# Collecting the scores of five scan levels in one column range: 80 predicated copies become 20, with three additions at level 6

## The reference

```
def step(s, inp):                      # one chunk of the prompt
    qc, kc, vc, gc = inp
    b = jnp.cumsum(gc, axis=2)
    diff = b[:, :, :, None, :] - b[:, :, None, :, :]
    decay = jnp.exp(jnp.where(tri[:, :, None], diff, NEG_BIG))
    att = jnp.einsum('bhtd,bhsd,bhtsd->bhts', qc, kc, decay)
    o = (jnp.einsum('bhts,bhsv->bhtv', att, vc)
         + jnp.einsum('bhtd,bhdv->bhtv', qc * jnp.exp(b), s))
```

## Time and profile before

| | us |
|---|---|
| median of 3 executions | 2847.42 (2844.85 to 2847.95) |
| the profiled execution, its own time | 2846.17 |
| its span, first to last instruction | 2844.4 |
| PE busy in the span | 2810.3 (99%) |
| DVE, ACT, POOL busy | 1689.4, 950.6, 1596.5 |
| granted TensorE clock, mean | 0.997 |

### The profile page before, as it was taken

One profiled execution on the slowest core, in us unless ns is written; L12 is line 12 of the kernel. 1 busy time (PEld: TensorE's weight loads), 2 busy tenths in 40 slices (PEclk: granted clock), 3 DMA queues, 4 the chain that ended last, 5 costly groups with the idle time before them and its releaser, 6 DMA issues.

```text
span 2844.4 us, 63198 instructions
## 1 busy us (share of the span) xinstructions
PE 2810.3 (99%) x24828; PEld 2766.3 (97%) x24828; DVE 1689.4 (59%) x2419; ACT 950.6 (33%) x1616; POOL 1596.5 (56%) x1466
## 2 busy tenths in 40 slices
PE   8999999999999999999999999999999999999998
PEld 7999999999999999999999999999999999999998
DVE  8554677545553578383784637766454446783645
ACT  4221233123152425151452414330412523452433
POOL 6666676556654674525464352766565556734343
PEclk9999999999999999999999999999999999999999
DMA  5796835665654655353444433355665557453532
GB/s 191 199 247 191 237 101 182 170 154 155 185 167 111 189 163 162 117 175 110 126 144 140 156 120 109 121 169 169 160 181 153 161 151 186 148 170 118 158 123 78
DMA packets 196956, 444.27 MB, mean 156 GB/s; under 512 B 13464, under 2 KB 57664, under 8 KB 195904
## 3 DMA queue, kind: packets, MB, share of 16 engines
q1 hardware_dynamic: 107360, 281.09, 30.4%
q0 software_dynamic: 40128, 125.83, 18.7%
q10 hardware_dynamic: 49248, 34.28, 4.0%
HBM read 422.64 MB, written 144.35 MB: 199 GB/s over the span
## 4 chain that ended last, share of the span: by engine, by line
PE 93%; DVE 3%; ACT 1%; POOL 1%; issue 1%; ACTq 0%; DVEq 0%; PEld 0%; POOLq 0%
PE dense L723 60%; PE SA L783 15%; PE SB L783 11%; POOL Wl L588 1%; PE SA L998 1%; PE SA L915 1%; PE SA L859 1%; PE SA L1001 1%; PE SA L903 1%; PE SA L846 0%; PE SA L920 0%; POOL Wh L586 0%; PE SB L1005 0%; PE SA L848 0%; PE SA L855 0%
## 5 line engine op out<-in xcount | busy, mean ns | idle before, releaser
L588 POOL TENSOR_TENSOR Wl<-raw,Wh 128x512 fp32r<-128x512 f32 x620 | 854.0, 1377 | 51.8
L586 POOL TENSOR_SCALAR Wh<-raw 128x512 fp32r<-128x512 f32 x620 | 450.9, 727 | 672.8 <-PEq L728 445.8
L723 PE MATMUL dense<-Hh,Wh 128*128 128x272 f32 x2768 | 585.8, 293 | 15.2 <-POOLq L590 10.1
L723 PE MATMUL dense<-Hh,Wl 128*128 128x272 f32 x2768 | 573.9, 289 | 0.5 <-issue 0.5
L723 PE MATMUL dense<-Hl,Wh 128*128 128x272 f32 x2768 | 572.6, 288 | 0.0
L723 PEld LDWEIGHTS dense<-Hh,Wh 128*128 128x128 f32 x2768 | 435.0, 189 | 25.7 <-issue 16.2
L723 PEld LDWEIGHTS dense<-Hl,Wh 128*128 128x128 f32 x2768 | 436.7, 189 | 0.0
L723 PEld LDWEIGHTS dense<-Hh,Wl 128*128 128x128 f32 x2768 | 434.0, 189 | 0.8 <-issue 0.8
L651 POOL TENSOR_TENSOR Sl<-pair,Sh 128x512 fp32r<-128x512 f32 x120 | 173.7, 1465 | 421.8 <-ACT Sh L1088 421.0
L723 PE MATMUL dense<-Ah,Wh 128*128 128x272 f32 x1408 | 291.9, 289 | 0.8 <-DVE X L1814 0.7
L723 PE MATMUL dense<-Al,Wh 128*128 128x272 f32 x1408 | 290.7, 288 | 0.0
(11 more groups left out here) (473 smaller groups left out, 6317.4 us busy)
## 6 DMA issues: line engine op xcount, KB each, us to landing
raw<-wst SPq DMA_DIRECT2D x276, 512.0 KB, 3.7
w_sums<-wst POOLq DMA_DIRECT2D x36, 1536.0 KB, 13.3
w_sums<-wst POOLq DMA_DIRECT2D x18, 2048.0 KB, 16.8
pair<-wst SPq DMA_DIRECT2D x120, 256.0 KB, 3.5
pair<-w_sums SPq DMA_DIRECT2D x60, 512.0 KB, 3.7
wsum<-w_sums SPq DMA_DIRECT2D x60, 512.0 KB, 3.6
w_sums<-w_sums POOLq DMA_DIRECT2D x12, 1536.0 KB, 9.0
wsum<-wst SPq DMA_DIRECT2D x60, 256.0 KB, 2.5
```

What stands on the lines that cost most here:

```text
L586: pool.tensor_scalar(Wh[:, j, cs], raw[:, j, cs], 1.0, 0.0, ALU.mult, ALU.add).then_inc(glink, 1)
L588: pool.tensor_tensor(Wl[:, j, cs], raw[:, j, cs], f32(Wh[:, j, cs]), ALU.subtract).then_inc(glink, 1)
L723: mm = pe.matmul(out[:, a, 0:HALF], w[:, ring, w0:w0 + 128], x[:, k, a * HALF:(a + 1) * HALF], start=(k == 0 and n == 0), stop=(k == nk - ...
```

## The change

Levels 1 to 5 no longer write to the four diagonal 32x32 blocks. One predicated copy on all 128 partitions writes all four groups' scores into the last 32 columns (96 to 127) of each block of `attC`. The last group of partitions has its diagonal block there already. At level 6, before its own copies, three additions of 32 partitions x 16 blocks x 32 columns add what groups 0 to 2 have collected to their diagonal blocks, where step `d` has written the diagonal; a sync of the chain stands behind them, since level 6 overwrites part of the collecting range. The mask that one copy needs must stand in the same 32 columns for all partitions, so three copies in `layer_bounds` of the first layer (32 partitions x 5 levels x 32 columns of bytes) bring the top-left mask block down to the other groups.

```diff
             def layer_bounds(L):
+                for j in range(1, 4 if L == 0 else 1):
+                    low, all_ = (lvm[g, 0:5 * P].rearrange("p (l t) -> p l t", t=P)[:, :, 0:32]
+                                 for g in (slice(0, 32), slice(32 * j, 32 * j + 32)))
+                    ch.did(dve.tensor_copy(all_, low))
                 ch.link(dve.tensor_copy(lbc[:, 0:4].unsqueeze(1), lbs[:, L:L + 1, :]))
...
                 elif kind == "lv":
                     dve.sem_inc(dve_began, 1)
                     bs, hf = 1 << h, 1 << (h - 1)
+                    for g in (slice(32 * j, 32 * j + 32) for j in range(3 if hf == 32 else 0)):
+                        ch.did(TT(attC[g, :, g], attC[g, :, g], attC[g, :, 96:P], ALU.add))
+                    if hf == 32:
+                        ch.sync()
                     for s0 in range(0, CH if hf >= 32 else 0, bs):
...
-                    for j in range(4 if hf < 32 else 0):
-                        g = slice(32 * j, 32 * j + 32)
+                    if hf < 32:
                         ch.did(dve.copy_predicated(
-                            attC[g, :, g].rearrange("p c (n b) -> p c n b", b=bs)[:, :, :, hf:bs],
-                            mask(h)[g, g].rearrange("p (n b) -> p n b", b=bs)[:, :, hf:bs].unsqueeze(1).to_broadcast(
-                                [32, HEADS * NCH, 32 // bs, hf]),
-                            SA[g, 0, 0:HEADS * NCH * 16].rearrange("p (c n b) -> p c n b", c=HEADS * NCH, b=hf)))
+                            attC[:, :, 96:P].rearrange("p c (n b) -> p c n b", b=bs)[:, :, :, hf:bs],
+                            mask(h)[:, 0:32].rearrange("p (n b) -> p n b", b=bs)[:, :, hf:bs].unsqueeze(1).to_broadcast(
+                                [P, HEADS * NCH, 32 // bs, hf]),
+                            SA[:, 0, 0:HEADS * NCH * 16].rearrange("p (c n b) -> p c n b", c=HEADS * NCH, b=hf)))
```

## The result

The changed kernel takes 2859.75 us (median of 6 runs, 2857.40 to 2861.42), the kernel before 2847.51 beside it. The ratio is 1.0038, 95% interval 1.0024 to 1.0051: slower, by about 12 us. The profiled execution has 2860.03 us, its span is 2858.2.

What follows compares the result with a forecast made beforehand. PE was taken to bound the kernel, busy 2810.3 of 2844.4 us. The terms -1.4 + 0.6 + 9.4 + 3.0 = +11.6 us, on 2847.42, gave 2859.0 us, range 2848 to 2866.

Steps and rivals of the forecast that it cites:

- Level 6 against POOL: Additions at level 6 push DVE's last three instructions into POOL's work; PE waits 2.2 and 2.5 us before level 7: +9.4 us.
- Levels 4 and 5: Shorter predicated copies let DVE finish before PE asks; the four waits of levels 4 and 5 in scan 0 go: -1.4 us.
- The mask copies: At about 121 us, first copy sits out POOL's block, three at 0.2 us follow while PE waits: +0.6 us.
- the lower of my two workings: Scan 1, level 6: old 2.64 us plus 1.5 for POOL's company, a 2.4 us wait; turn by turn 3.3.
- The clock: Behind the new waits ahead of level 7, PE at half clock in two of four cases: +3.0 us, bounds 0 and 6.
- The no-change rival: At level 6 only the additions' overrun of 0.6 and 0.35 us stays: 2848.5 us; chance 0.20.
- the waits without clock loss: Rival: the waits ahead of level 7 come but no half clock behind them: +8.6 us, 2856.0 us; chance 0.30.
- the wide copy as dear as four: Rival: one wide copy costs as much as four, levels 4 and 5 keep their 1.4 us: 2860.4 us; chance 0.06.

## Why the prediction was right

The forecast was 2859.0 us, +11.6; measured are 2859.75 and +12.2 of the medians (7 to 15 by the interval). The mechanism held. That the two numbers lie within 1 us of each other is in part luck. The profiled pair is 13.9 us apart, not 12.2. I had 12.4 us for what the additions cost (waits and clock) and 0.8 for what the rest gives back; by the medians the additions cost 14.3 us (from the kernel without them to the changed one) or 16.3 (put alone into the kernel before), and the rest gives back 2.1 to 4.1. Both sizes were too small, and their errors offset each other.

- **Level 6 against POOL** was the step that carried the sum, and it held: 9.4 us forecast, 9.0 measured, 1.97 in scan 0 and 2.55 in scan 1 for my 2.2 and 2.5. That the additions' own time isn't the cause is shown by two of them, which fit the margin and still cost 4.9 us of waits. The rule that I cited from the Trainium skill (SBUF — State Buffer, "Who interferes with whom") agrees with the turns in the timelines above: in scan 0, POOL's L588 of 578.70 lasts 2.13 us through L1953, and L1956 behind it 2.30. The turns are read from starts and ends; no run moved POOL's work itself. One detail of my working was off: the first addition of scan 1 would be blocked for 0.57 us; there, POOL had come earlier and DVE later, and the three additions lost 0.08. In turn POOL's company cost the last three lines of scan 1 2.04 us (4.68 for 2.64), where the lower of my two workings had 1.5. That the total came out the same was luck.
- **Levels 4 and 5**: -1.4 forecast, -1.0 measured; one wait of 0.44 stayed. The wide copy costs what a narrow one did (median 0.45 us for both):

```profile
L2022 DVE COPY_PREDICATED att<-lvm,SA x20: 435/452/746, 525.6 to 2145.9; 128x256 f32<-128x256 uint8 x20
```

- **The mask copies**: +0.6 forecast, 0.8 measured. The first sat out POOL's L588 (1.37 us), the two others took 0.25 each, as one line's min/median/max shows:

```profile
L1638 DVE COPY lvm<-lvm x3: 250/252/1368, 121.0 to 122.6; 32x160 uint8<-32x160 uint8 x3
```

- **The clock** was the term of least ground: two stretches of four (+3.0) forecast; three came, and with what went and came elsewhere the profile has +5.1. The stretches at 1848 and 2312 us of the profile after have no new wait ahead of them, and others of that kind come and go between kernels that don't differ there; I had no term for them. I had only the size of the wait to go by, and the size doesn't decide: half clock came behind the wait of 1.97 us at 1988 us and not behind the one of 1.96 us at 583 us, and behind both waits of 2.55 us here and neither of those in the kernel with each wide copy four times. In the kernel with two additions, whose longest wait was 1.42 us, it came behind none of the four.
- **The no-change rival** fell with the waits of 9.0 us (its bound was 6.5) and with the two-additions kernel; **the waits without clock loss** with the profile after, though the kernels with filling matmuls leave open how much of the 5.1 us is time; and **the wide copy as dear as four** with 0.45 us.

The loss can be had back in two ways, either of which is enough: moved by one step, or covered by one half tile, the same additions cost nothing.

## What to carry to other kernels

Work that is hidden under other engines' work is not free to move: compare its new place with the margin there, and ask what the instructions behind it will meet when they come later. Fewer and wider instructions gave 23 us of DVE time and 12 us of loss, because three short additions pushed the instructions behind them from a quiet stretch of POOL into a busy one. Where an engine idles right behind its signal to the one that sets the pace, put the extra work there, behind the signal and not ahead of it, as long as it ends before the next step is due: with DVE's shorter time at level 5 the additions fitted there, and without it they made two waits of 2.55 us.

## What the runs showed of the hardware that I had not expected

- Keeping PE busy with unused matmuls through a wait of some 2 us kept its full clock behind it in all four scans, and gave 2 to 3.5 us (within the intervals) with four matmuls and nothing with six, whose 2.91 us are longer than the waits. Standing still does not always cost it: of the eight waits of 1.96 to 2.78 us in the changed kernel and in the one with the additions alone, six have half clock behind them, and of the two of 2.55 us in the kernel with each wide copy four times, none.
- The kernel before scatters: 14 of its 77 runs lie more than 5 us above its median, up to 2858.28 us. Of the 67 runs of the seven kernels that do one wide copy a level (the changed one and six of its variants) none lies more than 5 us above its own median. The kernel with four narrow copies and three additions has two of eight, and one of them was the profiled one; the kernel with four narrow copies and two additions has none of ten. For 13 of the 14 a mean granted clock is on record, 0.993 to 0.997; for 58 of the others it is 0.995 to 0.998. The profiled run of the kernel with three additions shows PE's own issue standing still for 5.05 us inside level 4 of scan 0, and half clock behind it (timeline):

```profile
561.94 0.26 PE L915 MATMUL SA<-setA,kbuf 128*32 128x16 f32 x4 [5.05 <-issue]
```

The stretch of 4 us that holds it (windows):

```profile
559.00:563.00 4.00, 1.06 (x24) 1.02 (x25) 0.35 (x1) 0.00 (x0) 0.60 (x1) 0.50 0.19 52
```

- PE's stall inside level 2 of layer 0 is 1.66, 1.66 and 1.94 us in the profiles of the three kernels with narrow copies, and 0.71 to 1.03 in those of the changed kernel and of its variants with one wide copy a level. PE doesn't gain this time: in all those variants a second stall of 1.2 to 2.0 us stands inside level 4 of scan 0, at the place of the 5.05 us above, and of the kernels with four copies a level only that one profile has any there. The whole entry of PE's issue at L915 is 2.2 us before and 1.9 to 3.5 in the kernels with one wide copy a level. Both stalls lie at the same matmul of the program in every profile, behind the 109th of level 2 and the 106th of level 4, so something on PE's own side may set their place; no run tested it. What differs is the clock: half clock at 538 us follows the stall in the three kernels with narrow copies, in none of the others, and not in the kernel with each wide copy four times, whose stall was 1.94 us again. The variants with the additions behind level 5 and with the half tile beat the kernel before by 2.7 us, where the waits account for 0.6 us at most (1.4 gained, 0.8 lost); over the span they fall short of full clock by 3.4 us where the kernel before does by 6.8, and the rest should lie there. Why is open.
